# A hybrid decoder step on one core: input projection row by row with its steps' scan in the same stage, u kept on chip up to the experts, per-tile waits in the output projection, spreading begun after two turned tiles

## The reference

```python
u = rmsnorm(h, norm_mix)
p = u @ w_in
y_a, conv_new, ssd_new = ssd_group(p[..., :SSD_IN], ...)       # Mamba-2 heads; dt = softplus(dt_raw + dt_bias), decays exp(cumsum(dt * A))
y_b, shift_new, wkv_new = rwkv_group(p[..., SSD_IN:], ...)     # RWKV-7 heads
y = jnp.concatenate([y_a, y_b], axis=-1) @ w_out
h = h + y
h = h + peer(rmsnorm(h, norm_ffn), w_query, sub_keys, expert_u, expert_v)
```

## Time and profile before

| what | us |
|---|---|
| three runs | 4147.66, 4152.2, 4163.98 |
| median | 4152.2 |
| the profiled execution | 4144.62 |
| its span | 4143.1 |
| TensorE busy | 3678.9 (89%) |
| VectorE busy | 3276.2 (79%) |
| ScalarE busy | 1167.5 (28%) |
| GpSimd busy | 1225.3 (30%) |

### The profile page before, as it was taken

How to read it: one execution, slowest core, us unless ns; L and a number is a source line. 1 busy time by engine, 2 the same in 40 slices (tenths; PEclk the granted TensorE clock), 3 DMA queues, 4 the chain that set the end, 5 groups by cost and what they waited for, 6 DMA issues and landing times. The chain is left out here.

```text
span 4143.1 us, 65528 instructions
## 1 busy us (share of the span) xinstructions
PE 3678.9 (89%) x22408; PEld 3404.4 (82%) x22408; DVE 3276.2 (79%) x6456; ACT 1167.5 (28%) x2131; POOL 1225.3 (30%) x1079
## 2 busy tenths in 40 slices
PE   7997758888896888837779999999999999999997
PEld 6997747777785755537769999999999999999996
DVE  5542666676763489989969999999999999999998
ACT  3101343223221121239932222222222222222221
POOL 1121000000000000000035555565555555555552
PEclk9998679999997898969989999999999999999998
DMA  4784230000003010104478888888888888888885
GB/s 104 89 81 78 88 113 6 23 28 12 1 9 123 22 34 23 52 1 192 196 282 300 295 287 302 291 290 304 287 293 299 291 293 298 290 297 295 291 297 185
DMA packets 291717, 729.32 MB, mean 176 GB/s; under 512 B 27448, under 2 KB 138504, under 8 KB 290064
## 3 DMA queue, kind: packets, MB, share of 16 engines
q0 software_dynamic: 119296, 427.22, 33.4%
q1 hardware_dynamic: 172304, 300.64, 21.4%
HBM read 650.07 MB, written 77.70 MB: 176 GB/s over the span
## 5 line engine op out<-in xcount | busy, mean ns | idle before, releaser
L2735 POOL DMA_INDIRECT experts_u_row<-in_up_rows,experts_u_at x384 | 538.9, 1403 | 641.6 <-DVE experts_dot L2921 525.7
L107 PE MATMUL experts_down_ps<-experts_act_hi,experts_down_hi 128*128 128x352 f32 x2048 | 677.6, 331 | 9.2 <-DVE experts_down_lo L2897 6.8
L107 PE MATMUL experts_up_ps<-experts_u_hi,experts_up_hi 128*128 128x352 f32 x2048 | 662.2, 323 | 25.5 <-DVE experts_u_lo L2897 24.3
L108 PE MATMUL experts_down_ps<-experts_act_lo,experts_down_hi 128*128 128x352 f32 x2048 | 661.2, 323 | 0.0
L108 PE MATMUL experts_up_ps<-experts_u_lo,experts_up_hi 128*128 128x352 f32 x2048 | 660.9, 323 | 0.0
L109 PE MATMUL experts_up_ps<-experts_u_hi,experts_up_lo 128*128 128x352 f32 x2048 | 660.7, 323 | 0.0
L109 PE MATMUL experts_down_ps<-experts_act_hi,experts_down_lo 128*128 128x352 f32 x2048 | 660.6, 323 | 0.0
L2742 POOL DMA_INDIRECT experts_v_row<-in_down,experts_v_at x384 | 515.9, 1344 | 244.2 <-issue 103.0
L2921 DVE CUSTOM_DVE_ANT_0 experts_u_row<-experts_u_row,stream_u_rows_of 128x1024 f32<-128x1024 f32 x384 | 466.5, 1215 | 66.9 <-DMA experts_u_row<-in_up_rows,experts_u_at 65.4
L2934 DVE SCALAR_TENSOR_TENSOR stream_h_rows_of<-experts_v_row,experts_weight,stream_h_rows_of 128x1024 f32<-128x1024 f32 x384 | 497.9, 1297 | 14.5 <-DVE experts_weight L2926 6.6
L2940 DVE TENSOR_TENSOR stream_h<-stream_h,experts_down_ps 128x704 f32<-128x704 f32 x512 | 450.7, 880 | 72.3 <-PE experts_down_ps L109 69.6
(11 more groups left out here) (419 smaller groups left out, 6504.0 us busy)
## 6 DMA issues: line engine op xcount, KB each, us to landing
experts_up<-in_up SPq DMA_DIRECT2D x128, 512.0 KB
experts_down<-in_down SPq DMA_DIRECT2D x128, 512.0 KB
gates<-spread_spread SPq DMA_DIRECT2D x11, 4096.0 KB, 11.5
experts_gates<-gates SPq DMA_DIRECT2D x64, 704.0 KB
cols<-inp_done POOLq DMA_DIRECT2D x27, 576.0 KB
inp_w_in<-in_w_in SPq DMA_DIRECT2D x27, 512.0 KB
pick_w_query<-in_w_query SPq DMA_DIRECT2D x16, 512.0 KB
experts_u_row<-in_up_rows,experts_u_at POOLq DMA_INDIRECT x384
```

The lines of the kernel that those rows point to most:

```text
L107: pe.matmul(out, w_hi, x_hi, start=start, stop=False)
L108: pe.matmul(out, w_hi, x_lo, start=False, stop=False)
L2735: pool.indirect_dma_start(u_row[b][:], None, up_rows_d, bass.IndirectOffsetOnAxis(ap=u_at[slot][:, b, a:a + 1], axis=0)).then_inc(u_row_lo ...
```

## The change

- The steps' work (softplus, A, scan) moves from the start of the SSD stage into the input stage: tile 22 is now dt, tiles 23 to 26 the gates, written out instead of looped. ScalarE's Exp, Abs, Exp stand with tile 22 and Ln with tile 23. POOL stores 16 rows (dt and cum), after the scan and before the store of tile 23. The SSD stage loads them as one tile `dt_cum`; the 18 small matmuls become 9 of twice the width.
- Tile 0 of the input projection runs row block by row block over all three chunks; its weights are loaded second, behind x's first row.
- Output projection: waits by the tile two back, and the weights of tile 1 split before x is waited for.
- u stays on chip: its store and reload are gone. `down`, `u_row` and `v_row` of the experts lie in u's place, `up` and one `act_v` in `h_rest`'s. POOL's gathers and SP's `down` loads wait for `u_split`.
- Spreading starts after two turned tiles (the short one first); the last store is waited for by SP before the first gates are loaded, no longer at the stage's end; the first `up` tiles are loaded at the start of spreading.

```diff
-            body(lo, 0, 2 * lo, "dt")
+            body(lo, 0, DT_TILE, "dt")
+            for m in range(GATE0, IN_TILES):
+                body(m // 2, m % 2, m, "gate")
...
                 sp.dma_start(norm_g[:], norm_g_d).then_inc(g_loaded, 16)
-                for k in range(KD):
+                sp.dma_start(u[:, 0, :], x_t[0]).then_inc(x_loaded[0], 16)
+                sp.dma_start(w[0][:], w_pack[0]).then_inc(w_loaded[0], 16)
+                for k in range(1, KD):
                     sp.dma_start(u[:, k, :], x_t[k]).then_inc(x_loaded[k], 16)
...
+                    if isinstance(m, int) and m == 1:
+                        sp.dma_start(dt_par[:], dt_par_d).then_inc(par_loaded, 16)
+                        sp.wait_ge(u_split, START + KD)
+                        sp.wait_ge(sum_done, START + KD // 2)
+                        sp.dma_start(keep, keep_d[0:HEADS, :]).then_inc(par_loaded, 16)
...
-                        pool.wait_ge(gate_ready, START + GATE_TILES + 1)
+                        pool.wait_ge(dt_step, START + 6)
+                        pool.dma_start(cols_d[m, 0:2 * HEADS, :].rearrange("(a h) t -> h a t", a=2), u[0:HEADS, 0:2, :]).then_inc(stored[s], 16)
+                        return
...
                 for k in range(KD):
                     act.wait_ge(x_loaded[k], START + 16)
                     act.activation(u_hi[:, k, :], u[:, k, :], ACT.Copy, scale=norm_g[:, k:k + 1]).then_inc(u_rounded, 1)
-                    if k >= 4:
...
-                    act.activation(squares[:, k % 4, :], u[:, k, :], ACT.Square).then_inc(square_ready, 1)
...
+                    else:
+                        square(k - 1)
+                square(KD - 1)
...
+                    if k % 2 == 0 and k:
+                        add_pair(k - 1)
+                add_pair(KD - 1)
...
+                    if kind == "dt":
+                        for c in range(3):
+                            dve.wait_ge(proj_ready, START + m * 3 + c + 1)
+                            cols = slice(c * CH, c * CH + CH)
+                            last = dve.tensor_tensor(dt[:, cols], proj[s][0:HEADS, c, 0:CH], inv_rms[0:HEADS, cols], ALU.mult)
+                        last.then_inc(gate_ready, 1)
+                        dve.wait_ge(gate_ready, START + 1)
+                        dve.wait_ge(par_loaded, START + 32)
+                        dve.tensor_scalar(dt, dt, dt_par[:, 0:1], None, ALU.add).then_inc(dt_step, 1)
+                        return
...
+                    if kind == "gate" and m == GATE0 + 1:
+                        dve.wait_ge(dt_act, START + 4)
+                        dve.scalar_tensor_tensor(out=dt, in0=dt, scalar=0.0, in1=dt_abs, op0=ALU.max, op1=ALU.add).then_inc(dt_step, 1)
+                        dve.wait_ge(dt_step, START + 3)
+                        dve.memset(dt[:, NS:P - META], 0.0).then_inc(dt_step, 1)
+                        dve.wait_ge(dt_step, START + 4)
+                        dve.tensor_scalar(log_decay, dt, dt_par[:, 1:2], -1.0, ALU.mult, ALU.mult).then_inc(dt_step, 1)
+                        dve.wait_ge(dt_step, START + 5)
+                        dve.tensor_tensor_scan(cum, keep, log_decay, 0.0, ALU.mult, ALU.add).then_inc(dt_step, 1)
...
+                    if first:
+                        for k in range(KD):
+                            pe.wait_ge(u_split, START + k + 1)
+                            for c in range(3):
+                                one(c, k)
+                            if k % 2 == 0 and k:
+                                sum_of_squares(k - 1)
+                        sum_of_squares(KD - 1)
+                        return
...
-                pe.wait_ge(dt_step, 6)
+                pe.wait_ge(dt_loaded, 16)
...
-                        for a, src in enumerate((dt, cum)):
-                            for t in range(NT):
-                                mm = pe.matmul(small_ps[:, a, t, :], src[:, tile_cols(t)], eye[0:HEADS, 0:HEADS], start=True, stop=True)
+                        for t in range(NT):
+                            mm = pe.matmul(by_row_ps[:, t, :, :].rearrange("p a h -> p (a h)"), dt_cum[:, tile_cols(t)], eye[0:2 * HEADS, 0:2 * HEADS],
+                                           start=True, stop=True)
...
+                    if not isinstance(m, int) or m >= 2:
+                        pe.wait_ge(h_ready, START + q * 6 + 3 * s - 3)
...
-                    act.wait_ge(out_done, START + q * 6)
+                    if not isinstance(m, int) or m >= 2:
+                        act.wait_ge(out_done, START + q * 6 + 3 * s - 3)
...
+                split_w(1, 1)
                 dve.wait_ge(x_loaded, START + 32)
...
-                    else:
+                    elif not (isinstance(m, int) and m == 0):
                         split_w(1 - s, m + 1)
...
-                sp.wait_ge(u_ready, START + len(KEPT_CHUNKS) * KD)
-                sp.dma_start(u_d.rearrange("k p t -> p k t"), u[:, :, 0:DENSE]).then_inc(u_stored, 16)
-                sp.wait_ge(u_stored, START + 16)
...
+            if behind_first:
+                for s in range(2):
+                    group(0, s, s)
+                behind_first()
+            with eng.Fori(1 if behind_first else 0, ROW_GROUPS // 2) as q:
...
+                for e in range(SET):
+                    sp.dma_start(first_ups[e], up_d[e]).then_inc(first_ups_loaded[e], 16)
...
-                    sp.dma_start(at(gates_d, g), spread[s][:].rearrange("p j t -> p (j t)")).then_inc(stored[s], 16)
+                    done = last_stored if isinstance(g, int) and g == ROW_GROUPS - 1 else stored[s]
+                    sp.dma_start(at(gates_d, g), spread[s][:].rearrange("p j t -> p (j t)")).then_inc(done, 16)
...
-                    sp.wait_ge(stored[s], START + 16 * ((ROW_GROUPS + 1 - s) // 2))
+                    sp.wait_ge(stored[s], START + 16 * (ROW_GROUPS // 2))
...
+                dve.wait_ge(turned_out, START + 2)
...
+                over_groups(dve, nothing, batch, nothing, lambda: dve.wait_ge(turned_out, START + len(DENSE_TILES)))
...
+        up, act_v = first_ups, [spare, sb("act_v_1", [P, DENSE])]
...
+        place = u[:].rearrange("p k t -> p (k t)")
+        down, u_row, v_row = ([place[:, i * D:i * D + D] for i in which] for which in (range(SET), range(SET, SET + BLOCKS), range(SET + BLOCKS, SET + 2 * BLOCKS)))
...
-                for e in range(SET):
-                    sp.dma_start(up[e][:], up_d[e]).then_inc(up_loaded[e], 16)
-                for k in range(KD):
-                    if k >= 4:
-                        sp.wait_ge(u_split, k - 3)
-                    sp.dma_start(halves[k % 4], u_d[k]).then_inc(u_loaded[k], 16)
...
-                sp.wait_ge(u_split, KD)
+                sp.wait_ge(last_stored, 16)
                 for g in range(2):
                     load_gates(g, g)
                 for e in range(SET):
                     load_up(1, e)
+                sp.wait_ge(u_split, KD)
                 over_periods(sp, loads)
...
+                pool.wait_ge(u_split, KD)
                 over_periods(pool, fetches)
...
-                act.wait_ge(up_loaded[0], 16)
+                act.wait_ge(first_ups_loaded[0], 16)
                 act.activation(up_hi[0][:], up[0][:], ACT.Copy).then_inc(up_rounded, 1)
                 for k in range(KD):
-                    act.wait_ge(u_loaded[k], 16)
-                    act.activation(u_hi[:, k, :], halves[k % 4], ACT.Copy).then_inc(u_rounded, 1)
-                    if k == 0:
-                        act.wait_ge(up_loaded[1], 16)
+                    act.activation(u_hi[:, k, :], u[:, k, 0:DENSE], ACT.Copy).then_inc(u_rounded, 1)
+                    if k == KD - 1:
+                        act.wait_ge(first_ups_loaded[1], 16)
                         act.activation(up_hi[1][:], up[1][:], ACT.Copy).then_inc(up_rounded, 1)
...
-                    rest(u_lo[:, k, :], halves[k % 4], u_hi[:, k, :]).then_inc(u_split, 1)
-                    if k == 0:
-                        split_up(0, 1)
+                    rest(u_lo[:, k, :], u[:, k, 0:DENSE], u_hi[:, k, :]).then_inc(u_split, 1)
+                split_up(0, 1)
```

178 lines of the change are left out of this document (82 added, 96 removed).

## The result

The changed kernel takes 4083.9 us (median of four runs, 4081.3 to 4098.4) where the kernel before takes 4155.4 beside it: ratio 0.984, interval 0.982 to 0.986, that is 59 to 76 us less. Timed again in a later group it was 4061.6 against 4120.9, ratio 0.985 (0.982 to 0.987). The forecast was 4090, with 4072 to 4113 as its range. By the medians the gain is 71.5 us in the first group and 59.3 in the later one, where the sum said 61.9. The profiled execution has a span of 4080.4 us, against the 4143.1 before: 62.7 less, 0.8 more than the sum. Such a close hit has to be taken apart, since two errors can cancel. The table cuts both spans at the same events; the last column is the prediction's.

The account below looks back on a forecast made before the run. Experts' loop bound by TensorE (1924 of 1930 us busy), unchanged; elsewhere stages run one behind another, so path lengths count. 3.3 - 1.2 + 11.0 + 28.2 + 1.4 + 19.2 = 61.9 off the median 4152.2 gives 4090, range 4072 to 4113.

Parts of the forecast that it names:

- Input start: Input stage: TensorE starts tile 0 at about 11 and its work up to the mean ends 3.3 us sooner.
- The rest of the input stage: Input stage's gates: the steps' operations and POOL's stores stay hidden; only the last tile's Silu adds 1.2 us.
- SSD: SSD stage's start: TensorE waits only for constants and dt_cum, 7.1 us less; nine fewer small matmuls, 3.9 us less.
- Output projection: Output projection: pauses before tiles 1, 2, 4, 6 and the slow clock after them vanish, 28.2 us less.
- The reason that tile 2's weights come in time: Output projection: tile 2's weights are split by about 1315.5, while TensorE is in tile 1 until 1318.7.
- u's store: Picking stage: u's store lay beside VectorE's work, so taking it away gives nothing, 0 us.
- Spreading: Spreading's start: VectorE's first batch needs only the second copy; between bounds 0 and 2.6, 1.4 us less.
- Experts' start: Spreading's end to the experts: gates issued once the last store has landed, without u's reload, 19.2 us less.
- If `up` again takes 11.0: Experts' start: condition of the 19.2 us, that set 1's `up` lands 11.0 us after the first gates, as before.
- Rival 1: Transfers bind the experts' start, leaving 10.7 us there; output projection gains 20 instead of 28.2; 4107 us; chance 0.12.
- The 1.5 us: Experts' start: a third gather of 0.52 MB delays `up` by 1.5 us; not taken into the sum.
- Untouched stretches: Stages the change does not touch, and the experts' loop, keep their times, 0 us.

Follow-up runs that it names:

- the later pair of profiles: The kernel before and the changed kernel, both unchanged, profiled again in a later group; changed against before timed at ratio 0.985.
- its two halves: Changed kernel with tile 1's split late again: output projection 107.4 us; with the old pairwise waits instead: 114.2 us; changed kernel 96.5 us.
- the seven others: Seven later profiled kernels with the changed kernel's start of the experts: last store to gates 12.3 to 13.2 us, gates to set 1 17.6 to 18.5 us.

## Why the prediction was right, and where it was not

- **Input start, 3.3 said, 5.1 measured.** TensorE began at 10.99, near the 11.1 of the sum. The term was mis-sized in two places. I priced each of the four sums of squares at its recorded 2.20. From one group's start to the next (17.69 to 22.75) are 5.06 us, of which the 18 matmuls between take 3.12 at 0.173 each: a group costs 1.94, and only the last, which the mean waits for, its recorded 2.10. That is 0.9 too much. And the low clock cost 1.9, not 2.7: the first twelve matmuls took 4.0 us (10.99 to 15.00) where 2.1 would do.
- **The rest of the input stage, +1.2 said, +2.9 measured.** The last Silu costs 1.3 (last add to first load 6.3 before, 7.6 after, in both pairs). The other 1.6 lie in the waits for history, which scatter: in the later pair of profiles the last tile's add came 6.4 earlier, in the first 3.5. The steps' operations among the gates stayed hidden, though the longest wait was at another tile than argued.
- **SSD, 7.1 + 3.9 said, 6.6 + 3.9 measured.** Right, step by step.
- **Output projection, 28.2 said, 29.1 measured.** Right, and shown by its two halves. The reason that tile 2's weights come in time held: no pause before tile 2.
- **u's store, 0 said, 3.4 to 4.3 measured.** The step that failed: "taking it away gives nothing", because I looked at which engine's work lay beside the store, and not at VectorE's own wait that names no engine of the kernel. The row [6.57 <-remote] was in the trace, beside [3.22 <-remote] for the same instruction one pass earlier.
- **Spreading, 1.4 said, 1.7 measured.**
- **Experts' start, 19.2 said, 17.5 measured in this pair, 11.5 to 13.9 by the later profiles** (2044.0 less 2030.1 to 2032.5). The gates came 18.6 earlier, near the 19.2; the missing 0.6 is that the last store landed 12.2 us behind its issue, where the sum had the gates at 11.6. "If `up` again takes 11.0" is the step that failed: with three gathers ahead instead of two it took 12.9 here and 12.5 to 14.3 in the seven others. Set 1 started 3.2 us later behind the gates: 1.9 are `up`'s landing, and 1.3 are that from there to set 1 it took 5.2 instead of 3.9, VectorE's split standing behind the dots. Rival 1 named the mechanism, but its give-back of 8.5 was too large. The 1.5 us that I had worked out from the Trainium skill's page "DMA: Bandwidth & Descriptors", section "Issuing engines are not separate DMA queues", are near the 1.9 of the landing. What the low clock behind TensorE's new pause cost cannot be told: from set 1 to the end the changed kernel took 2.2 us less than the kernel before in the first pair and 1.0 more in the later one. So 17.5 is near 19.2 by luck; 13.7, as in the later pair, is the fairer figure.
- **Untouched stretches, 0 said:** RWKV +4.1 (within its 24 us of scatter), the rest of SSD -1.5.

The errors (-1.8, -1.5, -4.3, -0.9 and -0.3 on one side, +1.7, +0.5, +4.1 and +1.7 on the other, in us) nearly cancel; the sum's 0.8 us of agreement is better than its steps, and by the medians of the two groups the sum was 9.6 short and 2.6 over.

## What to carry over

Where two engines hand weights back and forth, look for waits that count in pairs and for splits that stand behind an unrelated load: here they were worth 29 us, over a third of it in the low clock behind each pause. An edit at a stage's start is kept only if the loop behind it is bound by the engine that you started earlier: ask what the other engines' loads and stores allow before you count it. Price a group of matmuls by the distance between starts, up to the next group's, not by its recorded length.

## What the runs showed of the hardware

- VectorE waits at each jump back to its loop's start, with one packet of the instruction queue moving: 3.1 to 3.5 us with the DMA engines otherwise idle, 5.6 to 6.6 beside a 2.8 MB store.
- The same 4188 matmuls with their waits took 706.8 to 730.5 us, with a mean granted clock of 0.89 to 0.86.
- The large stores of the input stage (576 KB, issued by GpSimd) took a median of 10.1 us in the changed kernel's first profile and 7.7 to 9.2 in all later ones. The input stage behind tile 1 was 24 us longer in the first profile of the kernel before than in its second, and 26 us in the changed kernel's: a loop that waits for such a store can be fast in one execution and not in another.
